# Hybrid decoder layer on one core: the first part's MLP from three fp32r products to one plain fp32 product, its down product over four chunks, and the top-k masks in two stages

## The reference, cut to what matters

```python
xn2 = rmsnorm(h, W['norm_ffn'][i])
g_conv, new_ffn = causal_dwconv(ffn_buf, xn2 @ W['w_gate'][i], W['conv_ffn'][i])
h = h + (jax.nn.silu(g_conv) * (xn2 @ W['w_up'][i])) @ W['w_down'][i]
...
score = jnp.where(causal[None], score, -jnp.inf)
_, sel = lax.top_k(score, n_sel)
```

## Time and profile before

| | us |
|---|---|
| time, median of 3 runs | 1925.38 (1919.97 to 1928.54) |
| the profiled execution | 1921.14 |
| its span, first to last instruction | 1919.5 |
| PE busy | 1699.0 (89%) |
| weight loads busy | 1528.4 (80%) |
| DVE busy | 1153.1 (60%) |
| ACT busy | 748.1 (39%) |
| POOL busy | 211.3 (11%) |
| mean granted clock of TensorE | 0.920 of full |

### The profile page before, as it was taken

How to read it: one execution, slowest core, us unless ns; L and a number is a source line. 1 busy time by engine, 2 the same in 40 slices (tenths; PEclk the granted TensorE clock), 3 DMA queues, 4 the chain that set the end, 5 groups by cost and what they waited for, 6 DMA issues and landing times.

```text
span 1919.5 us, 27805 instructions
## 1 busy us (share of the span) xinstructions
PE 1699.0 (89%) x9909; PEld 1528.4 (80%) x9909; DVE 1153.1 (60%) x2454; ACT 748.1 (39%) x1349; POOL 211.3 (11%) x356
## 2 busy tenths in 40 slices
PE   6989998987768888778999998799999999998894
PEld 5978897863557666556888898799999999997793
DVE  5456764386767876688655554455555555554544
ACT  4343443353568477723444432232222222225321
POOL 1000000121101212222633100000000000000000
PEclk9999999998867777878999999899999999999996
DMA  5321121331312222232323223112121212231002
GB/s 182 108 99 55 56 86 65 110 117 47 99 39 90 83 78 77 86 110 67 108 90 96 75 68 124 55 55 78 66 77 66 76 66 76 66 104 45 22 34 90
DMA packets 50226, 153.19 MB, mean 80 GB/s; under 512 B 9456, under 2 KB 12528, under 8 KB 50112
## 3 DMA queue, kind: packets, MB, share of 16 engines
q1 hardware_dynamic: 35248, 116.13, 17.7%
q0 software_dynamic: 14864, 35.60, 5.9%
HBM read 141.92 MB, written 9.76 MB: 79 GB/s over the span
## 4 chain that ended last, share of the span: by engine, by line
PE 55%; issue 12%; DVE 9%; ACT 5%; DMA 1%; POOLq 1%; POOL 1%; DVEq 0%; ACTq 0%
PE ps L1874 20%; PE ps L735 14%; PE ps L1975 8%; ACT act_junk L1230 3%; PE ps L1356 2%; PE ps L1396 2%; PE ps L1410 2%; PE ps L2141 1%; PE ps L1368 1%; PE ps L1422 1%; PE ps L1050 1%; DVE Pb_b L1605 1%; DVE wl L521 1%; DVE junk_b L1174 1%; DVE SC L1082 1%
## 5 line engine op out<-in xcount | busy, mean ns | idle before, releaser
L521 DVE TENSOR_TENSOR wl<-wr,wh 128x1024 fp32r<-128x1024 f32 x202 | 246.7, 1223 | 295.6 <-ACT wh L514 294.2
L514 ACT ACTIVATE wh<-wr 128x1024 fp32r<-128x1024 f32 x202 | 213.0, 1056 | 456.2 <-PE ps L1874 196.0
L1874 PE MATMUL ps<-xh_b,wh 128*128 128x336 f32 x832 | 264.7, 318 | 8.7 <-DVE xl_b L619 4.9
L1874 PE MATMUL ps<-xl_b,wh 128*128 128x336 f32 x832 | 265.1, 319 | 0.0
L1874 PE MATMUL ps<-xh_b,wl 128*128 128x336 f32 x832 | 263.4, 317 | 0.0
L735 PE MATMUL ps<-xh_a,wh 128*128 128x384 f32 x592 | 219.9, 372 | 22.7 <-DVE xl_a L619 8.4
L735 PE MATMUL ps<-xh_a,wl 128*128 128x384 f32 x592 | 217.5, 367 | 0.0
L735 PE MATMUL ps<-xl_a,wh 128*128 128x384 f32 x592 | 214.7, 363 | 0.0
L1874 PEld LDWEIGHTS ps<-xh_b,wh 128*128 128x128 f32 x832 | 157.6, 189 | 10.5 <-DVE wl L521 4.1
L1874 PEld LDWEIGHTS ps<-xh_b,wl 128*128 128x128 f32 x832 | 157.6, 189 | 0.0
L1874 PEld LDWEIGHTS ps<-xl_b,wh 128*128 128x128 f32 x832 | 157.2, 189 | 0.0
(11 more groups left out here) (365 smaller groups left out, 3432.5 us busy)
## 6 DMA issues: line engine op xcount, KB each, us to landing
wr<-in_weights SPq DMA_DIRECT2D x202, 512.0 KB, 3.5
pages<-in_d_pages POOLq DMA_DIRECT2D x128, 128.0 KB, 2.4
out_y<-TN SPq DMA_DIRECT2D x8, 528.0 KB, 2.7
pages<-in_c_pages POOLq DMA_DIRECT2D x128, 32.0 KB, 2.1
H<-in_xT SPq DMA_DIRECT2D x8, 336.0 KB, 9.3
H<-in_xT POOLq DMA_DIRECT2D x8, 336.0 KB, 5.4
H<-in_xT SPq DMA_DIRECT2D x8, 192.0 KB, 5.5
H<-in_xT POOLq DMA_DIRECT2D x8, 192.0 KB, 4.5
```

The costliest lines, as they stand in the source:

```text
L514: nc.scalar.activation(wh[:, slot], wr[:, slot], ACT.Copy).then_inc(w_hi, 1)
L521: nc.vector.tensor_tensor(wl[:, slot], wr[:, slot], wh[:, slot].bitcast(f32), ALU.subtract).then_inc(w_lo, 1)
L1874: last = nc.tensor.matmul(bank(first_bank + c)[:, 0:CB], w, x, start=k == 0 and t == 0, stop=k == KC - 1 and t == 2)
```

## The change

All products of the first part's MLP become plain fp32 matmuls: one for each tile, on the raw weights as SP loaded them and on unsplit rows. A gate or up quantum has 8 matmuls. The down product runs over four chunks: 5 groups with 8 quanta of 4 matmuls and a last group with 8 quanta of 2; the host packs the weights for it into new blocks of the same size. The splits of the 66 weight blocks (ACT and DVE), of the norm's rows and of the gate-times-up rows are gone; `PE` waits for the load itself. DVE's multiply writes straight to one of eight row buffers. `spread` now weighs a matmul by its length (a plain one 4 x 384, an fp32r one its columns). The halved convolution weights are made once. Array 2 (768 wide) of the search is counted by DVE in place of ACT. Each mask is cut into two stages (`need`, then `mask`), with a stage `found` for the thresholds ahead of them; in the plan the 31 steps end in item 58, `found` stands in item 59 and the last mask in item 66.

```diff
-ACT_TOP = [4, 3, 2, 1]
-DVE_TOP = [5, 0]
+ACT_TOP = [4, 3, 1]
+DVE_TOP = [5, 2, 0]
...
+SKIPPED = []
 def add_chunk(f):
     for kind in ("g", "u"):
         ORDER.append(ff_block(kind, f))
-        QUANTA.append((kind, f, 0, 24, len(ORDER) - 1))
-def add_down(g):
-    for half in range(2):
-        ORDER.append(ff_block("d", 2 * g, half))
-        QUANTA.extend(("d", g, 4 * half + m, 6, len(ORDER) - 1) for m in range(4))
+        SKIPPED.append(len(ORDER) - 1)
+        QUANTA.append((kind, f, 0, KC, len(ORDER) - 1))
+def add_down(g, part):
+    left = min(4, FC - 4 * g)
+    rows = 8 // left
+    ORDER.append(W_DA + 4 * g + part if left == 4 else ff_block("d", 4 * g, part))
+    SKIPPED.append(len(ORDER) - 1)
+    QUANTA.extend(("d", g, rows * part + m, left, len(ORDER) - 1) for m in range(rows))
...
+LENGTH = [{"d": 4 * NA, "g": 4 * NA, "u": 4 * NA, "pb": CB}.get(QUANTA[n][0], NA) for n, _ in MM]
...
-            + [("mask", NTOP - 1)] + [("mask", j) for j in range(NTOP - 1)])
+            + ["found"] + [(what, j) for j in [NTOP - 1, *range(NTOP - 1)] for what in ("need", "mask")])
...
             if j == 0:
-                pe.wait_ge(w_lo, s + 1)
+                if s in SKIPPED:
+                    pe.wait_ge(w_raw[s % 3], 16 * (s // 3 + 1))
+                else:
+                    pe.wait_ge(w_lo, split_no(s) + 1)
...
                 if kind == "d":
-                    pe.wait_ge(a_lo, 2 * f + 2)
+                    pe.wait_ge(a_mul, 4 * f + count)
             if kind == "d":
                 cols = slice(0, NA)
-                w, x = three(t, s % 3, (ah_a[:, (2 * f + k) % 3], al_a[:, (2 * f + k) % 3]), 4 * k + c % 4)
+                rows = 8 // count
+                w, x = wr[:, s % 3, rows * j + c % rows], gate_up_a(4 * f + j)
+            elif kind in ("g", "u"):
+                cols = slice(0, NA)
+                w, x = wr[:, s % 3, j], x_a[:, j]
...
         def act_dense(act, place):
...
-            for f in AH_AT.get(place, ()):
-                act.wait_ge(a_mul, f + 1)
...
-                nc.scalar.activation(ah_a[:, f % 3], gv_a[:, f % 2, 0:NA], ACT.Copy).then_inc(a_hi, 1)
...
         def dve_gate_mul(dve, link, f):
...
-            nc.vector.tensor_tensor(v, v, bank(6 + n % 2)[:, 0:NA], ALU.mult).then_inc(a_mul, 1)
+            nc.vector.tensor_tensor(gate_up_a(f), v, bank(6 + n % 2)[:, 0:NA], ALU.mult).then_inc(a_mul, 1)
...
-            nc.vector.memset(e[:, 0:2], 0.0)
-            link(nc.vector.tensor_scalar(w, p_("conv_ffn")[:, 3 * f:3 * f + 3], 0.5, None, ALU.mult))
...
-            def mask(self, dve, link, j, back=None):
+            def need(self, dve, link, j, back=None):
...
                 if back:
                     dve.wait_ge(*back)
                 link(self.count(j, sc, THR, ALU.is_gt))
                 nc.vector.tensor_scalar(equal, sc, self.col(THR, j, rows), None, ALU.is_equal)
                 link(nc.vector.tensor_scalar(self.col(NEED, j, rows), self.col(CNT, j, rows), -1.0, float(TOPK), ALU.mult, ALU.add))
+            def mask(self, dve, link, j):
...
                 link(nc.vector.tensor_tensor_scan(junk, run, equal, 0.0, ALU.mult, ALU.add))
```

More of the change, by code:

```diff
@@ L172, with spread @@
 assert 4 * (IDX_STEP + 6) == 4 * SIDX_STEP
-def spread(total, places):
-    weight = sum(w for _, w in places)
-    out, done = {}, 0
+def spread(first, last, places):
+    weight, total = sum(w for _, w in places), sum(LENGTH[first:last])
+    out, done, n, length = {}, 0, first, 0
     for place, w in places:
         done += w
-        out[place] = round(total * done / weight)
+        while n < last and length + LENGTH[n] / 2 <= total * done / weight:
+            length += LENGTH[n]
+            n += 1
+        out[place] = n
+    out[places[-1][0]] = last
     return out
 MM = [(n, j) for n, q in enumerate(QUANTA) for j in range(q[3]) if q[0] != "pa"]
+LENGTH = [{"d": 4 * NA, "g": 4 * NA, "u": 4 * NA, "pb": CB}.get(QUANTA[n][0], NA) for n, _ in MM]
 N_PB, N_OUT = 2 * NZ * 24, KC * 24
@@ L190 @@
 ISSUED = {}
[L191 to L194, removed]
+ISSUED |= spread(0, N_PB, [(p, 1) for p in range(0, 4 * PROJ_END)])
+ISSUED |= spread(N_PB, N_PB + N_OUT, [(p, 1) for p in range(4 * PROJ_END, NORM_AT - 4)])
+ISSUED |= spread(N_PB + N_OUT, len(MM), [(p, 1.0 if p < 4 * DSA_B else 1.2) for p in range(FFN_AT, NPOS)])
 for p in range(NPOS):
@@ L235 @@
     if kind == "u":
-        gate, down = Q_OF["g", f, 0], Q_OF["d", f // 2, 0]
+        gate, down = Q_OF["g", f, 0], Q_OF["d", f // 4, 0]
         last = min(last, limit(down))
@@ L700, in build, with split_no, gate_up_a @@
         LAST_A_UNIT = unit(A_END)
+        def split_no(s):
+            return s - sum(a < s for a in SKIPPED) if type(s) is int else s - len(SKIPPED)
+        def gate_up_a(f):
+            return gu_a[:, f % 8] if f % 8 < 6 else gu_rest_a[:, f % 8 - 6]
         def freed(n):
@@ L1584, in act_mixers @@
                 norm_ffn_a.act_stat(act)
-            if place in (NORM_AT + 3, NORM_AT + 4):
-                for k in range(4):
-                    norm_ffn_a.act_hi(act, k + 4 * (place - NORM_AT - 3))
         def dve_maxima(dve, link, n):
@@ L1739, in dve_mixers @@
                 k = 4 * (place - NORM_AT - 3)
-                norm_ffn_a.dve_split(dve, k, k + 4)
+                for k in range(k, k + 4):
+                    if k == 0:
+                        norm_ffn_a.until(dve, norm_ffn_a.bcast, 1)
+                    nc.vector.scalar_tensor_tensor(x_a[:, k], norm_ffn_a.src(k), norm_ffn_a.gain[:, k:k + 1], norm_ffn_a.factors,
+                                                   ALU.mult, ALU.mult).then_inc(norm_ffn_a.xn, 1)
         STORES = [("c_k", Z[0:HD, KC2], "ka", 0), ("c_idx", Z[0:HD, KI2], "ka", 0), ("c_v", Z[0:HD, CV], "cv", 0)]
@@ L2372, in weight_blocks @@
     out += [rows(w_ple_gate[:, m * P:(m + 1) * P]) for m in range(KC)]
+    for g in range(FC // 4):
+        w = w_down[4 * g * P:(4 * g + 4) * P].reshape(4, P, 4, 2, P)
+        out += [w[:, :, part].transpose(1, 0, 2, 3).reshape(P, KC, P) for part in range(4)]
     assert len(out) == NW
```

90 lines of the change are left out of this document (52 added, 38 removed).

## The result

The changed kernel takes **1866.79 us** (median, 1861.23 to 1869.50) beside 1926.96 for the kernel before: ratio 0.9688, 95% interval 0.9652 to 0.9724. The forecast was 1906, its lower end 1868. The gain is some 60 us, three times the one forecast. The profiled execution took 1866.3 us, its span 1864.6.

A forecast was written before the change was run, and what follows sets the result against it. PE bounds the sparse items, no engine is full in the search items, DVE is busiest in the mask items. +32 - 15 - 28 - 2 - 4 = -17 gave 1904 for the profiled execution, 1906 as median; range 1868 to 1958.

The forecast's parts named there:

- If half clock falls from a half to about a third of the time: Items 42 to 58: PE's 189 us of work would become some 225, about 255 with idle time.
- the longer down products: Down products: quanta taking two places each in place of one relax the bank swap, priced at 0.
- The last rival: MLP products: the weight load shows, four times 188 ns a record; +517 in place of +65, about 2360; chance 0.01.
- Sparse items: 913 to 1166 us: 278 dearer products add 34 us on PE's path, less 2 for remaining waits; net +32.
- Search items: Items 42 to 58, 516.9 to 787.1 us: relieved DVE and ACT, fewer waits; -15 (270 to 255), bounds -36 and +13.
- Rival (a): Differential items: fewer waits and longer products bring PE's clock back; net -41, 1884; chance 0.15.
- Mask items: Items 59 to 66, 787.1 to 913 us: 12.2 us stall goes, DVE's sum falls; -28, bounds -38 and +1.
- the wait for the 3.0 us fetch may remain in part: Items 59 to 66: work between the two mask stages covers the scores' fetch, perhaps not wholly.
- Sign items and norm: 480.6 to 516.9 us: three splits leave DVE, -2; norm ahead of the MLP: PE's 4.6 us split wait shrinks, -4.
- (b): Items 42 to 58: DVE becomes the bound, keeping 66 of 77 us of gaps; net -2, 1923; chance 0.17.
- (c): Items 42 to 58: PE becomes the bound at its slow clock, under about 0.79; +47, 1972; chance 0.18.
- (d): Items 59 and 60: mask stages don't free PE, a 12 us stall stays; net -5, 1920; chance 0.04.

The follow-up runs named there:

- e6: Changed kernel with down products over two chunks again, still plain fp32, so 88 residual sums in place of 48; 1884.55 us, ratio 0.9800.
- e10: Changed kernel with only DVE's 66 weight-block differences put back, results unused, ACT's copies left out; 1887.35 us, ratio 0.9805.
- e12: Kernel before with the MLP's part of the change alone, array 2 on ACT and one-stage masks as before; 1881.89 us, ratio 0.9808.
- e13: Changed kernel with the next item's page loads issued ahead of the scores' fetch in POOL's queue; 1862.5 us, ratio 0.9692.
- e2: Changed kernel with each mask in one stage again, thresholds in the first mask's stage; 1865.9 us, ratio 0.9696.
- e3: Kernel before with the new search alone: array 2 on DVE, masks in two stages, MLP as it was; 1915.2 us, ratio 0.9956.
- e4: Changed kernel with ACT and DVE again splitting all 66 MLP weight blocks, results unused and PE not waiting for them; 1896.9 us, ratio 0.9860.
- e14: Changed kernel with dense products spread evenly over places and page loads ahead of the scores' fetch in POOL's queue; 1859.57 us, ratio 0.9663.
- e11: Changed kernel with 176 gate and up products as three fp32r matmuls again and dense products spread evenly; 1867.82 us, ratio 0.9698.

## Why the prediction was wrong

The direction, the price of a product and the places were right; the forecast was 40 us too high. The step that failed most is in the search items, "If half clock falls from a half to about a third of the time": it fell to a fifth, and the stretch lost 33 us and not 15. The same kind of miss, half clock that went with the waits, is in the sparse and the sign items. And one term was put at nothing, the longer down products: undoing them in e6 costs 18 us.

For the profiled execution the forecast was 1904 us, and it took 1866.3. The 38 us between them are 18 in the search items, 14 in the sparse, 8 in sign items and norm, less 8 in the mask items, and 5 in the start, which have nothing to do with the change. There is a slip too: with the 4 us that the rivals have added, 1904 would be 1908 and not 1906.

**Price of a product: right.** 0.646 us against 0.645; the load stays hidden. The last rival (2360 us) falls. The Trainium skill ("TensorE: Matmul & The Clock Gate", weight-path perf modes) has the fast load off for fp32, and gives its theoretical four times for fp8. Read as a load four times as long for plain fp32 than for fp32r, it isn't what this trace shows: 190 ns for the loads of plain matmuls, and 190 for the second part's fp32r ones.

**Sparse items: +32 forecast, +18 measured** (+20 cut at PE's own matmul). That is under the 20 us that the forecast gave as a sign of being wrong, or just at it. The term 278 x 0.122 = 34 was right. What stood beside it was too small: "2 us for PE's few remaining waits (6 us idle in all)". PE's idle time fell by 5.4 us, and the half clock went altogether (0.97 to 1.00), which in 253 us is 7 us: 34 - 5 - 7 = 22, and 2 us stay unexplained beside the 20. The forecast took the clock of a full stretch as given, though 0.97 in 253 us was 14 us at half clock.

**Search items: -15 forecast, -33 measured.** DVE's sum was forecast at 204 and is 204.8; its wait for ACT's counts at under 10, and is 14.8. The sizing that failed is the next step, "If half clock falls from a half to about a third of the time": it fell to a fifth (0.90), and the idle time is 33 (forecast 31). PE's 189 us of work at that clock are 210, the 204 busy measured within 3%, and 210 + 31 is 241 where the forecast had 255. The stretch also lies in the bound with DVE alone, 234 to 244, but DVE isn't its only limit: 19 us more on DVE lengthen it by half of that (e10), and in e12 it took 241 us with DVE busy 166. Rival (a), the clock comes back, had the mechanism, and nearly the price in this stretch (-31), though at a clock of 0.95 that wasn't reached; its 1884 for the whole was still 17 us too high. It was given 0.15. A second step is refuted by e6: "The longer down quanta, two places each in place of one, relax the bank swap; 0." With short ones PE stands 20 us at dense products in these items, 8.7 of them for residual sums, and 18 us of the whole time come back.

**Mask items: -28 forecast, -20 measured** (-22 cut at PE's own matmul). The 12.2 us stall went as forecast. The step that failed is "the wait for the 3.0 us fetch may remain in part": it was looked for on DVE. DVE did wait 2.3 us for it. What held PE was on POOL, whose queue holds the next item's pages behind that very fetch. e13 prices it at 8 us with its half clock, and then the stretch is -30 in PE's stream. The reason given for the gain was wrong too: e2, with single masks, has the same time as the whole change. In the old MLP these items got 10 us shorter by the two stages and the three steps that leave (e3), and the search items 9 longer; in the new one the spared splits do that work, and a wait of 5 to 6 us is left either way. The late pages come with the two stages (e3 7.8 us, the changed kernel 4.7); in e2 and e12, with single masks, PE doesn't wait for them there.

**Sign items and norm: -6 forecast, -14 measured.** Three splits were priced at their own 3.7 us. With DVE busy 31.0 of 36.3 us, PE lost 6.4 us of idle time as well, and the half clock ended (0.88 to 1.00). With the splits back (e4) these items take 35.2 again. In the stretch ahead the norm's wait stayed:

```profile
PE ps L767 <- DVE x_a L1777: 4.7, 1, 4.7
```

The 4 us forecast for it didn't come; the 6 us that came are from other waits of PE there, one for ACT's index scores, which had 6.1 us before and has 0.8 now. Which of ACT's spared instructions did it wasn't tried.

**Rivals.** (b), DVE keeps its gaps: fell, as they shrank from 77 to 32 us. In e3, where DVE isn't relieved, they are 47 us, and the stretch doesn't shrink. (c), the slow clock and PE as the bound: its condition, a clock under 0.79, never arose. (d) had the right place; but the wait that is left is for pages, 4.7 us and not 12.

**What the misses share.** The forecast priced a wait at its own length and DVE's spared time as hidden unless it ended a wait. Two things were missing. A wait removed can take half clock along with it. And in items 39 to 66 DVE's time is close to the path though it is never full: in e10 it is busy 69 us more than in the changed kernel in the stretches from item 39 on. The 37 in the sparse items cost nothing. The other 32, in items 39 to 66, cost 3 + 9 + 6 = 18 us.

## What to carry to other kernels

Price a wait of TensorE at its length and half of the half-clock time that follows it, and count that as gained when the wait goes, unless another wait stands close by: in e13 that came out near (8 us for an estimated 11), in e14 not at all. Where an engine's relief and work moved onto it come in one change, price them together: here the search edits brought 8 us alone, and 23 after the MLP's (by the ratios; 15 by the medians). When a stall is removed, read the queue of the engine that stood in it, DMA issuers too, for what is issued behind it: that is late next.

## What the runs showed of the hardware

A wait of 3.8 us on TensorE was followed by 17.1 us at half clock though PE was busy 16.9 of them (e11), one of 4.7 us by 13.7 us (busy 13.0); with that wait gone, 3.4 were left (e13). In e14 a wait of 3.1 us was followed by 17.0 us at half clock (busy 15.6). The Trainium skill ("TensorE: Matmul & The Clock Gate", HAM oscillation) says that gaps bring the slow level back; the trace agrees, and it puts the greater part of such a wait's cost after the wait. A plain fp32 product of 384 columns costs 1.24 times three fp32r ones at full clock (0.646 to 0.522) and 1.33 times at half clock (1.28 to 0.96).
